# Causal scores of the first block: one float32 product per query tile, or two float32r products of stacked high and low parts

## The reference, cut to what matters

```python
s = jnp.einsum('bqghd,bkgd->bghqk', qb, kw) * scale
p = _masked_softmax(s - slopes * wd.astype(jnp.float32), wmask)   # slopes: one per head (ALiBi)
o_win = jnp.einsum('bghqk,bkgd->bqghd', p.astype(vw.dtype), vw)
...
o = gb[..., 0:1] * o_cmp + gb[..., 1:2] * o_slc + gb[..., 2:3] * o_win
```

## Time and profile before

| | us |
|---|---|
| median of 3 runs | 3386.72 |
| lowest, highest | 3381.82, 3387.19 |
| the profiled execution's own time | 3386.27 |
| its span | 3384.5 |

### The profile page before, as it was taken

How to read it: one execution, slowest core, us unless ns; L and a number is a source line. 1 busy time by engine, 2 the same in 40 slices (tenths; PEclk the granted TensorE clock), 3 DMA queues, 4 the chain that set the end, 5 groups by cost and what they waited for, 6 DMA issues and landing times.

```text
span 3384.5 us, 41352 instructions
## 1 busy us (share of the span) xinstructions
PE 3290.4 (97%) x15399; PEld 2631.6 (78%) x15399; DVE 1759.3 (52%) x2614; ACT 1298.7 (38%) x1849; POOL 212.3 (6%) x234
## 2 busy tenths in 40 slices
PE   8989998999999999999999999999999999999998
PEld 6667876888888888875688888878887668888887
DVE  7354478445553455435666555345553566555532
ACT  4226656223332333223256333333332325733322
POOL 1001100000000000000110100010000011010000
PEclk9959999999999999999999999999999999999999
DMA  5220022333333333333122333333333322233332
GB/s 126 88 57 4 1 57 75 100 94 93 99 94 94 98 93 93 98 89 83 51 52 67 90 99 98 92 91 105 93 93 95 81 57 46 64 94 93 99 92 64
DMA packets 518250, 275.12 MB, mean 81 GB/s; under 512 B 39523, under 2 KB 510408, under 8 KB 517987
## 3 DMA queue, kind: packets, MB, share of 16 engines
q1 hardware_dynamic: 513154, 262.77, 28.1%
q0 software_dynamic: 3600, 9.85, 1.1%
q10 hardware_dynamic: 1360, 0.66, 0.1%
HBM read 262.70 MB, written 2.14 MB: 78 GB/s over the span
## 4 chain that ended last, share of the span: by engine, by line
PE 90%; DVE 6%; ACT 2%; issue 1%; DMA 0%; DVEq 0%; POOL 0%; ACTq 0%; POOLq 0%
PE bank L375 25%; PE bank L376 24%; PE bank L377 24%; PE bank L1004 5%; PE bank L985 4%; PE bank L993 3%; PE bank L2392 1%; DVE wlo L351 1%; PE bank L2375 1%; PE bank L1688 1%; PE bank L2362 1%; DVE xc L1894 0%; DVE q L932 0%; PE bank L690 0%; PE bank L1707 0%
## 5 line engine op out<-in xcount | busy, mean ns | idle before, releaser
L375 PE MATMUL bank<-hhi,whi 128*128 128x512 f32 (+1 forms) x2504 | 991.9, 396 | 8.0 <-DVE wlo L351 5.0
L377 PE MATMUL bank<-hlo,whi 128*128 128x512 f32 (+1 forms) x2504 | 977.1, 390 | 0.0
L376 PE MATMUL bank<-hhi,wlo 128*128 128x512 f32 (+1 forms) x2504 | 977.0, 390 | 0.0
L351 DVE TENSOR_TENSOR wlo<-raw,whi 128x1024 fp32r<-128x1024 f32 x485 | 608.8, 1257 | 587.8 <-ACT whi L344 578.9
L344 ACT CAST whi<-raw 128x1024 fp32r<-128x1024 f32 x485 | 505.1, 1046 | 409.1 <-PE bank L377 394.8
L375 PEld LDWEIGHTS bank<-hhi,whi 128*128 128x128 f32 (+1 forms) x2504 | 470.5, 188 | 149.5 <-issue 45.1
L377 PEld LDWEIGHTS bank<-hlo,whi 128*128 128x128 f32 (+1 forms) x2504 | 470.4, 188 | 100.7
L376 PEld LDWEIGHTS bank<-hhi,wlo 128*128 128x128 f32 (+1 forms) x2504 | 470.6, 188 | 99.2 <-issue 3.4
L375 PE MATMUL bank<-uhi,whi 128*128 128x512 f32 x880 | 348.5, 396 | 0.0
L376 PE MATMUL bank<-uhi,wlo 128*128 128x512 f32 x880 | 348.0, 395 | 0.0
L377 PE MATMUL bank<-ulo,whi 128*128 128x512 f32 x880 | 348.0, 395 | 0.0
(11 more groups left out here) (447 smaller groups left out, 3598.8 us busy)
## 6 DMA issues: line engine op xcount, KB each, us to landing
raw<-in_ffn_w_gate SPq DMA_DIRECT2D x88, 512.0 KB, 3.9
raw<-in_ffn_w_up SPq DMA_DIRECT2D x88, 512.0 KB, 3.8
raw<-in_w_in SPq DMA_DIRECT2D x78, 512.0 KB, 3.8
raw<-in_ffn_w_down SPq DMA_DIRECT2D x64, 512.0 KB, 4.1
raw<-in_w_out SPq DMA_DIRECT2D x24, 512.0 KB, 4.1
raw<-in_ffn_w_down SPq DMA_DIRECT2D x32, 384.0 KB, 3.5
raw<-in_w_gate SPq DMA_DIRECT2D x22, 512.0 KB, 4.0
raw<-in_w_up SPq DMA_DIRECT2D x22, 512.0 KB, 3.8
```

The source lines that it names most:

```text
L351: k.nc.vector.tensor_tensor(k.wlo[:, slot, :], k.raw[:, slot, :], k.whi[:, slot, :].bitcast(F32), ALU.subtract)\
L375: mm(out, whi, hi(kc), start=start and i == 0, stop=False)
L376: mm(out, wlo, hi(kc), start=False, stop=False)
L377: last = mm(out, whi, lo(kc), start=False, stop=stop and i == kcs - 1)
```

## The change

It has five parts.

1. `normalize` writes a query chunk in one DVE instruction of 128x512; `q` now has 8 chunks of 128 rows, with two heads in each (`query_rows` tells rows and chunk). The zero fill on POOL goes away.
2. `kcmp` is written in two instructions of 64 rows, so that a group's other 64 rows stay at the zero they were set to.
3. The load of `dist` is issued on POOL with the other tables before `first_norms`; the wait for it right before the causal attention goes away.
4. The causal scores are two float32r products in place of one float32 product. For head h the stationary operand `qparts` has the high parts of the head's queries on its own 64 rows and the low parts on the other 64. The moving operands `kparts` are the keys' high parts on all 128 rows, and their low parts on all 128 rows.
5. These parts are made during the attention, ahead of use, by the two hooks: ACT makes the high part of a head's queries on step 8h for head h+1, and the high part of a group's keys on steps 32g+3 and 32g+11 for group g+1; DVE makes the rest on the same steps, after a wait for ACT. The first ones are made before step 0. ACT calls its hook with -1 for them; in the later layers this call does nothing.

```diff
-            for a, b, part in it.get("parts", [(0, rows, out)]):
-                last = nc.vector.scalar_tensor_tensor(out=part, in0=it["src"][a:b], scalar=it["gain"][a:b],
-                                                      in1=k.bank[5 - i % 2][a:b, :], op0=ALU.mult, op1=ALU.mult)
-            last.then_inc(*k.xn_done.up())
+            nc.vector.scalar_tensor_tensor(out=out, in0=it["src"], scalar=it["gain"], in1=k.bank[5 - i % 2][0:rows, :],
+                                           op0=ALU.mult, op1=ALU.mult).then_inc(*k.xn_done.up())
...
         todo = list(builds)
+        if on_act:
+            on_act(act, -1)
...
+                    pool.dma_start(dist[:, :], k.consts["dist"]).then_inc(*k.stage_landed.up(by=16))
...
+def query_rows(h):
+    g = h // HPG
+    return slice(HD * (g % 2), HD * (g % 2) + HD), g // 2 * HPG + h % HPG
...
-        for c in range(0, NH, HPG):
-            r = 64 * (1 - c // HPG % 2)
-            pool.memset(q[r:r + HD, c:c + HPG, :], 0.0).then_inc(*k.q_zero.up())
...
-        pool.dma_start(dist[:, :], k.consts["dist"]).then_inc(*k.stage_landed.up(by=16))
-        pool.wait_ge(*k.stage_landed.all())
...
+    stacked, keys = sb("qparts", [P, 2, T], F32R), sb("kparts", [P, 2, 2, 2, T], F32R)
...
-                steps=[dict(pairs=[(q[:, h, t * P:(t + 1) * P], kT[:, 2 * b + g // 2, 0:(t + 1) * P])],
+                steps=[dict(pairs=[(stacked[:, h % 2, t * P:(t + 1) * P], keys[:, g % 2, b, e, 0:(t + 1) * P])
+                                   for e in range(2)],
...
+    head_at = {8 * h: h + 1 for h in range(NH - 1)}
+    head_at[-1] = 0
+    keys_at = {32 * g + 3 + 8 * b: (g + 1, b) for g in range(NG - 1) for b in range(2)}
+    keys_at.update({-1: (0, 0), 0: (0, 1)})
...
+    def high_parts(act, t):
+        for g, b in [(0, 0), (0, 1)] if t == -1 else [keys_at[t]] if t > 0 and t in keys_at else []:
+            rows, _ = query_rows(HPG * g)
...
+            nc.scalar.copy(keys[rows, g % 2, b, 0, :], kT[rows, 2 * b + g // 2, :]).then_inc(*k.k_high.up())
+        if t in head_at:
...
+            nc.scalar.copy(stacked[rows, h % 2, :], q[rows, c, :]).then_inc(*k.q_high.up())
+
+    def low_parts(dve, t):
+        if t in keys_at:
...
+            dve.wait_ge(*k.k_high.at(order.index((g, b)) + 1))
+            nc.vector.tensor_copy(hi[other(rows)], src)
+            for to in (rows, other(rows)):
+                last = nc.vector.tensor_tensor(lo[to], src, hi[rows].bitcast(F32), ALU.subtract)
+            last.then_inc(*k.k_parts.up())
+        if t in head_at:
...
+            dve.wait_ge(*k.q_high.at(h + 1))
+            nc.vector.tensor_tensor(stacked[other(rows), h % 2, :], q[rows, c, :], stacked[rows, h % 2, :].bitcast(F32),
+                                    ALU.subtract).then_inc(*k.q_parts.up())
+
+    attention(k, groups, mem, builds, ready=ready, splits=low_parts, on_act=high_parts)
```

More of the change, by code:

```diff
@@ L1455, in _ @@
         dve.wait_ge(*k.small_ready.all())
[L1457 to L1460, removed]
+    items = [dict(norm=c, rows=P, src=raw_queries(otok, c), out=q[:, c, :], gain=gain) for c in range(KC)]
     items += [dict(norm=KC + c, rows=P, src=kT[:, c, :], out=kT[:, c, :],
@@ L1463, in first_norms, with causal_attention @@
     normalize(k, items, back, *scales[1:], NORM1_HEADS)
-def causal_attention(k, mem, q, kT, vals, gates, otok):
+def causal_attention(k, mem, q, dist, kT, vals, gates, otok):
     nc = k.nc
[L1470 to L1474, removed]
-        pool.dma_start(dist[:, :], k.consts["dist"]).then_inc(*k.stage_landed.up(by=16))
-        pool.wait_ge(*k.stage_landed.all())
+    sb = lambda name, shape, dt=F32: mem.enter_context(nc.sbuf_tensor(k.name(name), shape, dt))
+    bias = sb("bias", [P, 2, T])
+    stacked, keys = sb("qparts", [P, 2, T], F32R), sb("kparts", [P, 2, 2, 2, T], F32R)
     handover(k)
@@ L1489, in causal_attention @@
                 out=otok[:, :, h * HD:(h + 1) * HD], add=True, factor=gates[:, :, 3 * h + 1 + b]))
-    attention(k, groups, mem, builds)
+    other = lambda rows: slice(HD - rows.start, P - rows.start)
+    head_at = {8 * h: h + 1 for h in range(NH - 1)}
+    head_at[-1] = 0
+    keys_at = {32 * g + 3 + 8 * b: (g + 1, b) for g in range(NG - 1) for b in range(2)}
+    keys_at.update({-1: (0, 0), 0: (0, 1)})
+    order = [keys_at[t] for t in sorted(keys_at)]
+    ready = {8 * h: [k.q_parts.at(h + 1)] for h in range(NH)}
+    for g in range(NG):
+        for b in range(2):
+            ready.setdefault(32 * g + 4 * b, []).append(k.k_parts.at(order.index((g, b)) + 1))
+    def high_parts(act, t):
+        for g, b in [(0, 0), (0, 1)] if t == -1 else [keys_at[t]] if t > 0 and t in keys_at else []:
+            rows, _ = query_rows(HPG * g)
+            if g >= 2:
+                act.wait_ge(*k.qk_done.at(32 * (g - 1)))
+            nc.scalar.copy(keys[rows, g % 2, b, 0, :], kT[rows, 2 * b + g // 2, :]).then_inc(*k.k_high.up())
+        if t in head_at:
+            h = head_at[t]
+            rows, c = query_rows(h)
+            if h >= 2:
+                act.wait_ge(*k.qk_done.at(8 * (h - 1)))
+            nc.scalar.copy(stacked[rows, h % 2, :], q[rows, c, :]).then_inc(*k.q_high.up())
+    def low_parts(dve, t):
+        if t in keys_at:
+            g, b = keys_at[t]
+            rows, _ = query_rows(HPG * g)
+            src, hi, lo = kT[rows, 2 * b + g // 2, :], keys[:, g % 2, b, 0, :], keys[:, g % 2, b, 1, :]
+            dve.wait_ge(*k.k_high.at(order.index((g, b)) + 1))
[4 more added lines that the diff above has]
+        if t in head_at:
+            h = head_at[t]
+            rows, c = query_rows(h)
+            dve.wait_ge(*k.q_high.at(h + 1))
+            nc.vector.tensor_tensor(stacked[other(rows), h % 2, :], q[rows, c, :], stacked[rows, h % 2, :].bitcast(F32),
+                                    ALU.subtract).then_inc(*k.q_parts.up())
+    attention(k, groups, mem, builds, ready=ready, splits=low_parts, on_act=high_parts)
 def turn_split(k, tok, hi, lo, copied, read, added):
@@ L1661, in _ @@
         by_block = lambda t: t[:, 0:cols].rearrange("p (n g) -> p n g", g=NG)
-        nc.vector.scalar_tensor_tensor(out=kcmp[:, :, 0:NCMP].rearrange("p g n -> p n g"), in0=by_block(kraw),
-                                       scalar=vector(k, "k_norm_g")[:, 0:1], in1=by_block(kroot), op0=ALU.mult,
-                                       op1=ALU.mult)
+        for e in range(2):
+            rows = slice(HD * e, HD * e + HD)
+            nc.vector.scalar_tensor_tensor(out=kcmp[rows, e::2, 0:NCMP].rearrange("p g n -> p n g"),
+                                           in0=by_block(kraw)[rows, :, e::2], scalar=vector(k, "k_norm_g")[rows, 0:1],
+                                           in1=by_block(kroot)[rows, :, e::2], op0=ALU.mult, op1=ALU.mult)
         dve.wait_ge(*k.cmp_v.at(1))
```

9 lines of the change are left out of this document (4 added, 5 removed).

## The result

The changed kernel is slower: 3412.47 us, the median of 4 runs (3409.22 to 3414.76), against 3384.27 of 4 runs before. The ratio is 1.0082, with an interval of 1.007 to 1.0094. The direction was forecast, the size was not: +28 us instead of +9, and the time lies 1.5 us above the upper end of the range, 3411. The profiled execution took 3413.07 us, with a span of 3411.3 (before 3386.27 and 3384.5).

The account below looks back on a forecast made before the run. The prediction took PE, busy 97% of the span, as the bound. It summed -5.4 us at full clock, +13.7 for the clock and 0.5 for second waits to +8.8, hence 3395.5 us, range 3379 to 3411.

Parts of the forecast that it names:

- query norms: Norms before the attention: 8 full instructions for 16 halves, 1.03 us per chunk, 8.3 us instead of 12.3: -4.0 us.
- wait for `dist`, 2.9 for the first parts: Opening of the causal attention: earlier load saves 3.1 us; making first key and query parts before the first score costs 2.9.
- loop and second parts at full clock: Causal attention loop: 173.2 us against 175.7, so -2.5, plus 1.3 for DVE's second set of parts.
- clock in the loop: PE's clock in the causal attention: falls at some pauses, 40 us at 0.50, +13.7 us net; thought to decide the sign.
- second waits: Causal attention loop: small second waits behind a pause, +0.5 us.
- The scores on PE: Causal scores as float32r pairs: 1.42 us instead of 2.38 per four steps, -30.7 us over 16 heads without waits.
- Rival D: Float32r pairs of 128 columns or row-crossing casts slower than assumed; +0.05 on each pair is 3 us more; chance 0.05.
- PE stands still for 1.2 us once a head: Causal attention: chain through ACT's copy and cast and DVE's query part takes 2.86 us against 1.64 of PE work.
- Rival A: Clock stays up after the causal attention's start: -5.4 us, 3381, up to 5 us less possible; chance 0.24.
- Rival B: DVE keeps its lead in the causal attention, each head 9.06 us: -34 us, 3353; chance 0.05.
- Rival C: Clock down for half the causal attention or more, over 80 us at 0.50: +24 and up, 3411 to 3430; chance 0.13.

Follow-up runs that it names:

- e2: Changed kernel with ACT's casts removed, DVE making the high parts too on the same steps: 3358.45 us, ratio 0.9916 to the kernel before.
- e1: Changed kernel with DVE's parts, and their wait for ACT, four steps later in its list, ACT's casts unmoved: 3359.22 us, ratio 0.9923 to the kernel before.
- e10: Changed kernel with all its parts and waits, but scores as one float32 product of raw chunks (two heads mix): 3418.39 us, ratio 1.0111 to the kernel before.
- e3: Changed kernel with eight unread float32r products of 252 columns on PE where it would pause, waits kept: 3391.64 us, ratio 1.0023 to the kernel before.
- e8: Changed kernel with both the edit of e1 and that of e5: 3359.74 us, ratio 0.993 to the kernel before.
- e9: e2 with two unread float32 products of 512 columns on PE ahead of the first scores: 3354.05 us, ratio 0.9905 to the kernel before.
- e5: Changed kernel with ACT's build of the next head's bias three steps later, away from the cast: 3421.07 us, ratio 1.0102 to the kernel before.

## Why the prediction was right in direction and wrong in size

| term | forecast us | measured us |
|---|---|---|
| query norms | -4.0 | -4.9 |
| wait for `dist`, 2.9 for the first parts | -0.2 | -2.7 |
| loop and second parts at full clock | -1.2 | about +9 to +11.4 |
| clock in the loop | +13.7 | +17.5 to +20 |
| second waits | +0.5 | in the loop |
| later layers | 0 | +5.5 |
| sum | +8.8 | +26.8 |

The step that failed is the third row, the loop with its pauses: -1.2 us was forecast at full clock, and it cost 9 to 11.4. That is over half of the 18 us by which the sum is off. The clock's term was 4 to 6 us too small on top of it, and the later layers, put at nothing, took 5.5.

**The query norms held.** Of the -4.9 us, 0.4 had come about before the first of these products. The chain has 24 products in 12.38 us for 12 chunks, two per chunk, so 1.03 per chunk for queries and keys alike:

```profile
194.83 12.38 PE bank L804 x24
```

**The scores on PE held.** The chain counts 0.23, 0.41 and 0.52 us for pairs of 128, 384 and 512 columns (forecast 0.22, 0.40, 0.51), and a group is 4.58 us instead of 4.53. Rival D fell with that. A little over 29 us of PE's work do go away, and e2 collects nearly all of them.

**"PE stands still for 1.2 us once a head" was the step that failed first.** The mechanism was right, and e1 and e2 show it: take the wait out of DVE's list and the pause goes. The size was not. From 300.86 to 304.24 is 3.38 us instead of 2.86. Against the same 1.65 us of PE's work that leaves 1.73 instead of 1.2 (the other 0.05 of the head's 1.78 come a step later). Three links were costed too short, as the chain and this timeline of ACT show:

```profile
300.36 0.63 ACT L1026 ACTIVATE bias<-dist 128x512 f32<-128x512 f32 x1
300.90 0.39 ACT L1032 ACTIVATE prob<-biased,low 128x128 f32<-128x128 f32 x1
301.19 0.57 ACT L1039 COPY probT<-bank 128x512 f32<-128x512 f32 x1
301.79 0.61 ACT L1507 CAST qparts<-q 64x512 fp32r<-64x512 f32 x1
303.68 0.51 ACT L1032 ACTIVATE prob<-biased,low 128x256 f32<-128x256 f32 x1 [1.28 <-DVE low L1078]
```

The copy starts 0.33 us behind PE's transposes and not 0.10, since ACT is still at a bias build and an exponential. The cast starts 0.60 us behind the copy's start, where the forecast had an exponential's 0.48. The bias starts 0.72 us behind the query part (0.62 was taken). From the bias to the transposes it is 1.09 us (303.15 to 304.24), where 1.02 was taken. 15 heads x 0.5 is 8 us. The group's 0.05 adds 16 x 0.10 = 1.6. A change of keys costs 1.84 beyond a head's pause in e10, which has no filler, where 1.7 was forecast. The longer opening at 0.50 adds 1.4. From the forecast -1.2 this comes to +10.6; e3 gives +11.4, or 9 without the filler's own cost. The 1.4 are clock, which the forecast had in its clock term; put there, they leave 7.6 to 10 for the pauses.

**The clock term was the largest, as forecast,** and was sized by choice: "40 us", between bounds of 0 and 90. It was 59.3. But it did not decide the sign. The forecast had a gain of 5.4 us at full clock, which the clock would turn into a loss. The measured rows without the clock's and without the later layers come to +1.4 to +3.8: there was no gain to turn. So the direction came out right in part by luck. The price of a microsecond, 0.40, was about right: 51.1 us beyond e3's time at 0.50 cost 17.5 to 20, or 0.34 to 0.39 each. That the clock would fall at some of the pauses was borne out. Rival A was a clock that stays up, with 5.4 us gained: e3 holds the clock up and is not faster than before but 0.23% slower. Rival B is what e1 and e2 build: -27 us where -34 was forecast. Rival C's 3411 came nearest in time, but by other terms; 59 us are not the 80 that it needed.

The Trainium skill, page "TensorE: Matmul & The Clock Gate", section "Why this matters for your kernels", puts drops down to idle gaps longer than any seen here. The trace disagrees: the longest idle before a score in the loop is 1.9 us in the waits above. The same table has the clock swing for thin matmuls that are not kept together ahead of the next load. On waits among thin products the trace agrees: the change, with pauses in its thin mix, has 59.3 us at 0.50, and e1 and e2, without them, have 4.8 and 8.3, at the opening.

**Two terms were missing.** The compressed attention now met a higher clock near its end (0.78 over 245:257, where the earlier trace rows has 0.50), 4.9 us earlier in time than before. From the first product of L1688 to the end of the last one of L1707 it takes 44.5 us instead of 46.6, so 2.1 of the extra 2.5 us before the first score. It can't be put down to the change as such: e2 and e10, whose code is the same up to there, were at 0.50 to its end, and it took them 46.6 us. Its last eight products with the values, before and after:

```profile
256.09 3.75 PE L1707 MATMUL bank<-vcmp,cpT 128*128 128x256 f32 x8 [0.80 <-ACT cpT L1724]
...
250.85 2.00 PE L1745 MATMUL bank<-vcmp,cpT 128*128 128x256 f32 x8 [1.22 <-ACT cpT L1762]
```

And the mixers of later layers open with a longer stretch at 0.50, though nothing in them was changed. These are the windows of their opening, of before and of after:

```profile
1694.00:1760.00 66.00, 60.19 (x426) 54.12 (x427) 46.89 (x112) 35.60 (x72) 14.14 (x15) 0.97 0.27 51
```

```profile
1715.00:1780.00 65.00, 58.51 (x393) 52.53 (x394) 45.08 (x107) 32.53 (x66) 14.02 (x15) 0.92 0.26 52
```

0.97 is 4 us at 0.50 and 0.92 is 10; by the place of the same product in both traces it cost 3.2 us there. The mixers of the layer after show the same (0.97 over 2800:2866 before, 0.92 over 2822:2888 after) and cost 2.9; the rest of the later layers comes to -0.6. e1, e8 and e9, whose attention has hardly a pause, show 10 us at 0.50 at the first of these openings, and e2 24; e3 and e10, which have the pauses, show 3.4, as before. So it doesn't come from the attention's pauses; why it came was not tried.

**What stays open:** why ACT's cast doesn't start before its copy has ended; whether e5, with a slightly shorter pause, had the clock down for longer by its edit or by chance (its four runs have mean clocks of 0.969 to 0.972, the four of the change 0.971 to 0.974); and which of the pauses brings it down.

## What to carry to other kernels

Here, a wait put into the list of an engine that runs ahead cost the whole lead, and not just the work behind it. Before moving a part of a job to a second engine, follow the chain both ways: 0.42 us saved on an engine with time to spare bought a pause of 1.7 us on the one that is the bound. If the part must cross engines, make it several steps before it is asked for, as e1 does. And a small pause on PE can cost more than its length where its products are thin: here the loop lost 17.5 to 20 us more to the clock.

## What the runs showed of the hardware beyond that

- The clock's fall did not need a long gap. With pauses of 1.3 to 1.9 us on a thin mix it was at 0.50 for 59 us of 207. With products of no use in the same pauses it was at 1.00 for all but the opening, and that was worth 17.5 us of the loop at least.
- The same pauses with float32 scores had 19 us at 0.50, and the thin mix without pauses 5 to 8, the opening included.
- On ACT an exponential and a copy behind it start 0.29 us apart where the first one's record is 0.39 long. Between a copy of 0.57 and the float32r cast behind it are 0.60: they did not overlap.
- The clock at an opening can differ by several us between kernels that are alike there: the compressed attention (0.78 and 0.50 over 245:257) and the later mixers (10 and 4 us at 0.50). A few us of any difference between these kernels can be that.
